# Products on x times its weight beside a norm, and gate weights spread through the merge: one change to a two-block transformer kernel

## The reference

```python
gates = jax.nn.sigmoid(gl + b_merge[l]).reshape(Bn, L, N_BRANCH, D_MODEL)
merged = (gates[:, :, 0] * (y_fox @ w_proj_fox[l])
          + gates[:, :, 1] * (y_s5 @ w_proj_s5[l])
          + gates[:, :, 2] * (y_mem @ w_proj_mem[l]))
x = x + merged @ w_out[l]
...
return rms_norm(x, g_final)          # y = x * rsqrt(mean(x*x) + eps) * g
```

```python
ada = c_act @ w_ada[l] + b_ada[l]
sh1, sc1, gt1, sh2, sc2, gt2 = [a[:, None, :] for a in jnp.split(ada, 6, axis=-1)]
h = rms(x, g_mix[l]) * (1.0 + sc1) + sh1
parts = jnp.split(h @ w_in[l], IN_SPLITS, axis=-1)
...                                   # attention A and B on the parts: y_a, y_b
gate_a = jax.nn.sigmoid(parts[3 + 3 * N_B])
gate_b = jax.nn.sigmoid(parts[4 + 3 * N_B])
x = x + gt1 * ((gate_a * y_a + gate_b * y_b) @ w_out[l])
h2 = rms(x, g_mlp[l]) * (1.0 + sc2) + sh2
x = x + gt2 * (jnp.square(jax.nn.relu(h2 @ w_ff1[l])) @ w_ff2[l])
```

## Time and profile before

| what | value |
|---|---|
| median of three runs | 2289.02 us (2288.14 to 2290.26) |
| profiled execution, its own time | 2291.23 us |
| its span (first to last instruction) | 2289.4 us |
| mean granted TensorE clock | 0.992 |
| instructions | 31094 |
| PE busy | 2249.8 us (98%) |
| POOL busy | 1691.9 us (74%) |
| DVE busy | 1259.3 us (55%) |
| ACT busy | 632.8 us (28%) |

### The profile page before, as it was taken

One profiled execution on the slowest core, in us unless ns is written; L12 is line 12 of the kernel. 1 busy time (PEld: TensorE's weight loads), 2 busy tenths in 40 slices (PEclk: granted clock), 3 DMA queues, 4 the chain that ended last, 5 costly groups with the idle time before them and its releaser, 6 DMA issues.

```text
span 2289.4 us, 31094 instructions
## 1 busy us (share of the span) xinstructions
PE 2249.8 (98%) x11693; PEld 1828.1 (80%) x11693; DVE 1259.3 (55%) x1798; ACT 632.8 (28%) x1286; POOL 1691.9 (74%) x2678
## 2 busy tenths in 40 slices
PE   8999999999999999999999999999999999999999
PEld 6888677788887888777778888878877777888887
DVE  7986345554446665544867576457554456723221
ACT  3233344332224111543223233111144421300000
POOL 7998170867888798344889887889853387899884
PEclk9999999999999899999999999999999999999999
DMA  7456741334455332111545555533321132433221
GB/s 204 129 137 153 268 151 35 116 101 159 159 186 186 111 111 94 50 36 39 164 131 189 174 191 177 184 107 97 100 79 33 29 124 92 154 107 107 92 92 56
DMA packets 268656, 280.87 MB, mean 123 GB/s; under 512 B 29964, under 2 KB 240592, under 8 KB 268508
## 3 DMA queue, kind: packets, MB, share of 16 engines
q1 hardware_dynamic: 249756, 245.86, 34.8%
q10 hardware_dynamic: 18752, 33.03, 4.3%
HBM read 257.87 MB, written 17.85 MB: 120 GB/s over the span
## 4 chain that ended last, share of the span: by engine, by line
PE 85%; POOL 6%; DVE 4%; issue 2%; ACT 2%; DMA 1%; SPq 0%; ACTq 0%; DVEq 0%; POOLq 0%
PE ps L496 46%; PE ps L674 14%; PE ps L2527 4%; PE ps L2528 4%; PE ps L2529 4%; POOL ring_low L272 4%; POOL ring_high L268 3%; PE ps L982 2%; PE ps L1025 2%; PE ps L1001 2%; PE ps L1175 1%; PE ps L1182 1%; PE ps L1158 1%; PE ps L2637 1%; DVE ada_acc L408 1%
## 5 line engine op out<-in xcount | busy, mean ns | idle before, releaser
L272 POOL TENSOR_TENSOR ring_low<-ring,ring_high 128x256 fp32r<-128x256 f32 x1309 | 1039.0, 824 | 28.4
L268 POOL TENSOR_SCALAR ring_high<-ring 128x256 fp32r<-128x256 f32 x1309 | 609.1, 491 | 478.3 <-PE ps L674 170.8
L496 PE MATMUL ps<-hT_high,ring_high 128*128 128x512 f32 x704 | 278.0, 395 | 1.4 <-DVE hT_low L860 1.4
L496 PE MATMUL ps<-hT_low,ring_high 128*128 128x512 f32 x704 | 274.9, 390 | 0.0
L496 PE MATMUL ps<-hT_high,ring_low 128*128 128x512 f32 x704 | 274.0, 389 | 0.0
L674 PE MATMUL ps<-hT_high,ring_high 128*128 128x512 f32 x568 | 234.5, 413 | 3.2 <-POOL ring_low L272 1.4
L674 PE MATMUL ps<-hT_high,ring_low 128*128 128x512 f32 x568 | 225.3, 397 | 0.0
L674 PE MATMUL ps<-hT_low,ring_high 128*128 128x512 f32 x568 | 225.1, 396 | 0.0
L408 DVE TENSOR_REDUCE ada_acc<-ring 128x256 f32<-128x2048 f32 x48 | 188.8, 3933 | 54.8 <-ACT ring L395 54.7
L496 PE MATMUL ps<-hidden_high,ring_high 128*128 128x512 f32 x512 | 201.0, 393 | 0.0
L496 PE MATMUL ps<-hidden_low,ring_high 128*128 128x512 f32 x512 | 199.6, 390 | 0.0
(11 more groups left out here) (401 smaller groups left out, 4030.5 us busy)
## 6 DMA issues: line engine op xcount, KB each, us to landing
ring<-in_w_in_dram SPq DMA_DIRECT2D x75, 1024.0 KB, 5.3
ring<-in_w_ff_dram SPq DMA_DIRECT2D x64, 1024.0 KB, 5.4
ring<-in_w_ada_dram SPq DMA_DIRECT2D x48, 1024.0 KB, 5.4
ring<-in_w_out_dram SPq DMA_DIRECT2D x12, 1024.0 KB, 5.8
scratch_x<-xT ACTq DMA_DIRECT2D x3, 2048.0 KB, 8.2
ring<-in_w_mem_kv_dram SPq DMA_DIRECT2D x4, 1024.0 KB, 5.4
ring<-in_w_branch_a_dram SPq DMA_DIRECT2D x16, 256.0 KB, 4.0
xT<-scratch_x ACTq DMA_DIRECT2D x2, 2048.0 KB, 9.7
```

The costliest lines, as they stand in the source:

```text
L268: ins = nc.gpsimd.tensor_scalar(x(hi), x(raw), 1.0, 1.0, ALU.mult, ALU.mult)
L272: ins = nc.gpsimd.tensor_tensor(x(lo), x(raw), x(hi).bitcast(F32), ALU.subtract)
L496: return nc.tensor.matmul(out[0:rows, bank, cols[0]:cols[1]], lhsT, rhs, start=start, stop=stop)
```

## The change

In the stage ahead of each norm, ACT and DVE also write x times its weight (its gain), without the root, as high and low parts into `hT` (class `Unnormed`). `norm_stage` lets PE multiply the first tile of the stage behind the norm by these; at the double norm it is two tiles. Beside each block's products stand two small products of the same weights with the shift's high and low part, in two columns (`shift_of`). Turn and spread are put between the blocks. When DVE has made the normed blocks, it scales the finished tiles by the spread root; the shift's sum is added as a bias by ACT's tanh or relu. The dummy products go, and the sums are turned in one bank with fewer matmuls.

The first tiles are those of gate slab `m{l}0ga`, which moves ahead of the qkv slabs, and at the MLP norms the first of ff. In layer 1 the second gate tile runs beside the first group of qkv. So the stream has 14 tiles for 16, and the paces are lower: attention A is fed 8 matmuls a step for 9, attention B 10 for 14.

Ada slabs move: the merge gets five more (iterations 3, 5, 7, 9 and 11, between gate and branch slab, keyed to the gate slab's first half) and `ada_lag` 2; out of the first block keeps two of four, out of layer 0 none of three. In out, the sums of squares are added ahead of a tile, not behind it. Mix doesn't wait for the whole stream at its entry, only ahead of its fourth tile. At the MLP norm the normed blocks pass through two PSUM banks instead of SBUF.

The core of the diff:

```diff
@@ -348,27 +348,31 @@
     for mp in range(4):
         for b, (pw, rows) in enumerate((("w_proj_fox", 768), ("w_proj_s5", 768), ("w_proj_mem", 512))):
             add(f"merge{mp}{b}g", w, dm, O_GL + D * b, D, part=mp)
+            one = (len(K.slabs) - 1, 1)
+            if 3 * mp + b in (3, 5, 7, 9, 11):
+                ada(0, 0)
             add(f"merge{mp}{b}p", T[pw][0], (0, rows), 0, D, part=mp)
-            one, other = (len(K.slabs) - 2, 1), (len(K.slabs) - 1, 0)
...
             ada(0)
     for i in range(4):
         add("out", T["w_out"][0], dm, 0, D, part=i)
-        ada(0)
+        if i < 2:
+            ada(0)
...
+        add(f"m{l}0ga", w2, dm, 3072, D, part=0)
...
-            add(f"m{l}{mp}ga", w2, dm, 3072, D, part=mp)
+            if mp:
+                add(f"m{l}{mp}ga", w2, dm, 3072, D, part=mp)
...
         for i in range(4):
             add(f"out{l}", T["w_out_2"][l], dm, 0, D, part=i)
-            if l == 0 and i < 3:
-                ada(0)
...
+    v, hi = K.nc.vector, K.shift_two[:, :, 0]
+    K.link(e, "dve_step", v.tensor_copy(hi, shift))
+    K.link(e, "dve_step", v.tensor_tensor(K.shift_two[:, :, 1], shift, hi.bitcast(F32), ALU.subtract))
+
...
+class Unnormed:
...
+    def round_up(self, e, k):
+        K = self.K
+        K.nc.scalar.activation(K.hT[0][:, k, :], self.src[:, k, :], ACT.Copy, scale=self.gain[:, k:k + 1]
+                               ).then_inc(self.high.sem, 1)
+    def low_part(self, e, k):
+        K = self.K
+        e.wait_ge(self.high.sem, self.base + k + 1)
+        K.nc.vector.scalar_tensor_tensor(K.hT[1][:, k, :], self.src[:, k, :], self.gain[:, k:k + 1],
+                                         K.hT[0][:, k, :].bitcast(F32), ALU.mult, ALU.subtract).then_inc(self.low.sem, 1)
...
+            def products_of(k):
+                pe.wait_ge(unnormed.low.sem, unnormed.base + k + 1)
+                for n, t in enumerate(tiles):
+                    if k == 0:
+                        K.weight_here(pe, t[0][5])
+                    for x in range(3 * k, 3 * k + 3):
+                        _, rows, cols, lhsT, rhs, _, start, stop = t[x]
+                        ins = nc.tensor.matmul(ps[0:rows, tile_banks[n], cols[0]:cols[1]], lhsT, rhs, start=start, stop=stop)
+                ins.then_inc(used.sem, 1)
+            def shift_of(n, k):
+                for x in (3 * k, 3 * k + 2):
+                    ins = nc.tensor.matmul(ps[:, shift_bank, 2 * n:2 * n + 2], tiles[n][x][3], K.shift_two[:, k, :],
+                                           start=x == 0, stop=x == 3 * KD - 1)
+                if (n, k) == (len(tiles) - 1, KD - 1):
+                    ins.then_inc(made.sem, len(tiles))
+            def turn(bank, parts):
+                for t in range(TT):
+                    for n, x in enumerate(parts):
+                        ins = nc.tensor.matmul(ps[:, bank, t:t + 1], x[:, t * P:(t + 1) * P], K.ones[:, 0:1],
+                                               start=n == 0, stop=n == len(parts) - 1)
+                ins.then_inc(turned.sem, 1)
...
+            pe.wait_ge(taken.sem, taken.total - 2)
+            for k in range(KD):
+                products_of(k)
+                if twice is not None:
+                    squared, summed = twice[0]
+                    for h in (2 * k, 2 * k + 1):
+                        shift_of(h // KD, h % KD)
+                    if k == 1:
+                        pe.wait_ge(taken.sem, taken.total)
+                        pe.wait_ge(summed.sem, summed.total)
+                        pe.wait_ge(squared.sem, squared.total - 1)
+                        turn(turn_bank, (sums, last))
+                    if k == 3:
+                        pe.wait_ge(inverted.sem, i0 + 1)
+                        spread_root(root_bank, 4)
+                    if k == 4:
+                        pe.wait_ge(squared.sem, squared.total)
+                        turn(other_bank, (twice[3], twice[4]))
+                    if k == 6:
+                        pe.wait_ge(inverted.sem, i0 + 2)
+                        spread_root(other_bank, 1)
+                else:
+                    shift_of(0, k)
+                    if k == 2:
+                        pe.wait_ge(taken.sem, taken.total)
+                        turn(turn_bank, (sums, last))
+                    if k == 4:
+                        pe.wait_ge(inverted.sem, i0 + 1)
+                        spread_root(root_bank, 4)
...
+                pe.wait_ge(copied.sem, c0 + 1)
...
             low_part(KD - 1)
+            K.link(e, "dve_step", v.tensor_copy(rstd[:, :], ps[:, root_bank, :]))
+            e.wait_ge(made.sem, made0 + len(tiles))
+            for n in range(len(tiles)):
+                K.link(e, "dve_step", v.tensor_reduce(K.shift_of[:, n:n + 1], ps[:, shift_bank, 2 * n:2 * n + 2], AX_X, ALU.add))
+                take(e, n, ps[:, tile_banks[n], :], rstd[:, :])
...
     tiles_stage(K, merge_tiles(K, branches, 4, names), 2, act=act, dve=dve, tensor_entry={}, entry_at=(2, tensor_entry),
-                waits=waits)
+                waits=waits, ada_lag=2)
...
+    unnormed = Unnormed(K, xq, K.gains[:, 3, :])
+    def first_gains(e, n):
+        if n == 0:
+            mix_gains(K, e, 0)
...
+        if n >= 1:
+            unnormed.low_part(e, n - 1)
...
+                if g == 1:
+                    pe.wait_ge(*gates_scaled)
...
                             pe.wait_ge(arriving[0].sem, arriving[1] + k + 1)
+                        if g == 0 and beside is not None and k < KD // 2:
+                            if k == 0:
+                                K.weight_here(pe, beside[0][0][5])
+                            for j in (2 * k, 2 * k + 1):
+                                pe.wait_ge(arriving[0].sem, arriving[1] + j + 1)
+                                for _, _, _, lhsT, rhs, _, start, stop in beside[0][3 * j:3 * j + 3]:
+                                    ins = nc.tensor.matmul(K.ps[:, beside[1], :], lhsT, rhs, start=start, stop=stop)
+                            if k == KD // 2 - 1:
+                                ins.then_inc(beside[2], 1)
...
+    for n in range(2):
+        K.weight_used((gate_slab, n), gates_made.sem, gates_made.total + n + 1)
+    def scale_gates(e, n, ps, rstd):
+        v.tensor_tensor(scaled_gates[n][:, :], ps, rstd, ALU.mult)
+        v.tensor_scalar(K.half_shift[:, n:n + 1], K.shift_of[:, n:n + 1], 0.5, None, ALU.mult).then_inc(gates_scaled.sem, 1)
...
     if l == 0:
-        xq, squared, sums, last = K.outer
-        arriving = norm_stage(K, xq, gains[:, 3, :], K.hT, ada[:, 0:8], sums[1], last[1],
-                              (squared, K.g_final, K.xT, sums[0], last[0]), banks=(2, 3, None))
+        places = ((1, 2), 4, 0, 3, 5, None)
+        xq, unnormed, squared, sums, last = K.outer
+        arriving = norm_stage(K, xq, gains[:, 3, :], K.hT, ada[:, 0:8], sums[1], last[1], unnormed, first_gates, places,
+                              gates_made, scale_gates, (squared, K.g_final, K.xT, sums[0], last[0]))
     else:
...
-            tiles += column_tiles(K, K.first[f"m{l}{mp}g{b}"], 2, KD, K.hT)
-
...
+            if mp or b == "b":
+                tiles += column_tiles(K, K.first[f"m{l}{mp}g{b}"], 2, KD, K.hT)
+    stream = Stream(K, tiles, [(6, 5, 7)[(n + 1) % 3] if n < 9 else 6 + n % 2 for n in range(14)],
+                    lambda e, n, ps: nc.scalar.activation(gates[n + 2], ps, ACT.Tanh, scale=0.5))
...
+    def turn_gates(e):
+        e.wait_ge(gates_scaled.sem, gates_scaled.total)
+        for n in range(2):
+            shift = {"bias": K.half_shift[:, n:n + 1]} if n < ahead else {}
+            nc.scalar.activation(gates[n], scaled_gates[n][:, :], ACT.Tanh, scale=0.5, **shift).then_inc(gates_turned.sem, 1)
...
     attention_stage(K, steps, [probs[:, k] for k in range(4)], [turned[:, k] for k in range(2)], gate_slab, stream,
-                    [72 + 9 * i for i in range(18)] + [240, 252])
+                    [72] + [85 + 8 * i for i in range(17)] + [220, 226])
...
     wide_attention_stage(K, steps, [probs[:, k] for k in range(3)], [t[:, :, :] for t in turned], stream,
-                         [(252, 252, 274)] + [(278 + 14 * i, 284 + 14 * i, 288 + 14 * i) for i in range(7)] + [(376, 382, 384)])
+                         [(226, 226, 246)] + [(249 + 10 * i, 254 + 10 * i, 256 + 10 * i + 8 * (i == 6)) for i in range(7)] + [(328, 334, 336)])
...
-    tiles_stage(K, tiles, 2, dve=mix_dve, also=mix_high, waits={(0, 0): (al.sem, al0 + 4), (0, 12): (yl.sem, yl0 + 2)})
+    tiles_stage(K, tiles, 2, dve=mix_dve, also=mix_high, tensor_entry={x: y for x, y in before.items() if x != "stream"},
+                entry_at=(3, {"stream": before["stream"]}), waits={(0, 0): (al.sem, al0 + 4), (0, 12): (yl.sem, yl0 + 2)})
...
     def mlp_gain(e, n):
-        if n == KD - 1:
...
+        else:
+            unnormed.low_part(e, n - 1)
...
+    def out_high(e, n):
+        if n < KD - 1:
+            e.wait_ge(added.sem, added0 + n + 1)
```

(32 more changed lines are left out.)

180 lines of the change are left out of this document (95 added, 85 removed).

## The result

The changed kernel takes 2296.68 us (median of 20 executions, 2291.04 to 2300.80) against 2289.69 for the kernel before (2286.22 to 2292.38): a ratio of 1.0028, 95% interval 1.0021 to 1.0035, so slower by some 6.5. The forecast was 2286 with a range from 2271 to 2296, so the median lies 0.7 above the range, and the time moved the other way. The changed kernel's profiled execution took 2291.04, the least of the twenty, with a span of 2289.3, hardly other than before (2289.4). I therefore took two more profiles of the same kernel; the third execution (2295.22) is nearest to the median, and the text reads both.

The account below looks back on a forecast made before the run. PE, busy for 98% of the span, was taken as the bound, with gaps at the norms. Gains of 21.3 against 18.5 for moved ada slabs gave -2.8 on 2291.23, taken over to the median 2289.02: 2286 us, range 2271 to 2296.

Parts of the forecast that it names:

- MLP norm, layer 1: Layer 1's MLP norm: the same gain as in layer 0, with its half-clock gap, -4.0 us.
- the price of the moved ada slabs: Merge and out: regular ada slabs wait in the three-slot ring for POOL's gate split; 18.5 us lost, between 8 and 24.
- The falls of the clock: Lower clock after long waits: 2.8 us at merge iteration 5; the second out sum's 5.2 also included a fall.
- The upper bound of 24: Upper end of the forecast loss from the moved ada slabs in merge and out, taken as 18.5 us.
- The double norm: Between out and qkv: gate, shift, turn and spread products fill PE's gap; new stretch 19.8 us, gain 8.6.
- Layer 1's norm: Norm of layer 1's mix: gap of 6.66 becomes 9.9 us, second gate tile beside qkv; net +0.2.
- Layer 0's MLP norm: Tile 0 done in the gap, normed blocks some 1.9 later, tile 2 ends at 21.05 for 24.95: -3.9 us.
- Layer 0's out: Loses its three ada slabs, with a POOL wait of 2.2 and three sums at 0.25: -2.9 us.
- Attention and the entry of mix: Thinner filler costed at nothing in A, B's last step -0.6 us; mix no longer waits for the last gate, -1.5.
- (B): Merge has more slack, landing or split some 3 us sooner: loss 8 for 18.5, 2275 to 2276 us; chance 0.24.
- (C): POOL becomes the bound at the norms, slowed by DVE's low-part passes: 9 us in all, 2295; chance 0.16.
- (D): Attention loses its cover with fewer filler products a step: some 3 us a layer, 2292; chance 0.10.

Follow-up runs that it names:

- the dummy products: The changed kernel with dummy products of 256 columns (4, 7, 4 and 8) ahead of the merge's four long waits for ada sums: 2296.24 us.
- the order of the slabs: The changed kernel with the five extra ada slabs issued ahead of their gate slab, not behind it: 2289.86 us, ratio to before 0.9998.
- the kernel with the ada slabs nearly where they were: Changed kernel, two extra ada slabs in merge (iterations 5, 11, ahead of gate slab), three in layer 0's out, its MLP norm as before: 2285.26 us, ratio 0.9976.

## Why the prediction failed, step by step

The prediction's terms and what they measured, as differences of the table above (first profile, third):

| term | predicted | first | third |
|---|---|---|---|
| merge and out | +18.5 | +23.4 | +25.4 |
| double norm, layer 0's attention and entry of mix | -9.65 | -11.1 | -9.3 |
| out, layer 0 | -2.9 | -3.2 | -3.25 |
| MLP norm, layer 0 | -3.9 | -3.1 | -1.7 |
| norm, attention, entry of mix, layer 1 | -0.85 | -1.3 | -1.2 |
| MLP norm, layer 1 | -4.0 | -4.3 | -4.4 |
| sum | -2.8 | +0.3 | +5.7 |

**The step that failed is the price of the moved ada slabs:** 18.5 in the sum, 23.4 and 25.4 measured. Its mechanism was right, chain and place: iteration 5 was put at a wait of 4.6 and waited 4.3 to 4.6 in three profiles. But iterations 3 and 9 waited 2.7 to 2.8 and 2.5 to 2.6 for 1.3 and 1.4, iteration 11 kept 4.7 to 5.6 *and* a wait of 2.27 at the start of out, where I had set the one off against the other, and the second sum of out waited 2.4 to 2.7. That is 4.7 of waits short in the first profile, of a miss of 4.9. The falls of the clock I added on top, 2.8 twice; for the one in the merge the dummy products show that this was the wrong kind of term: taking the falls away there gave nothing back. I priced wait by wait, each from its own starting tile; the dummy products and the order of the slabs speak for a ring, in which a late slab makes the next one late. The upper bound of 24 was closer than the value taken.

**The double norm** came out as worked out in the first profile: 20.18 where 19.8 stood, of which 0.99 is a wait for POOL and the rest PE's own work:

```profile
765.30 0.39 PE L827 MATMUL ps<-hT_high,ring_low 128*128 128x512 f32 x1
766.68 0.50 PE L827 MATMUL ps<-hT_high,ring_high 128*128 128x512 f32 x1 [0.99 <-POOL ring_low L272]
...
767.25 0.39 PE L827 MATMUL ps<-hT_high,ring_low 128*128 128x512 f32 x1
767.48 0.16 PE L833 MATMUL ps<-shift_two,ring_high 128*128 128x2 f32 x1
...
767.84 0.48 PE L827 MATMUL ps<-hT_high,ring_high 128*128 128x512 f32 x1
```

Four shift products and the start of the next block's product take 0.36 + 0.09, so 0.11 each, at the 0.12 that was taken from the nearest row. The Trainium skill, "TensorE: Matmul & The Clock Gate", section "Wait — 56ns, not 53.3ns?", has a floor of about 25 ns for small matmuls; the rows are over four times that. What I left out: in two of three profiles the clock falls in the middle of this stretch, and of layer 0's MLP norm, and they are 1.4 to 1.9 longer each. Layer 1's norm was put at 9.9 at clock 1; up to the first product of the tile beside qkv it is 11.1 to 11.4 in the three profiles, with a fall in each, and 9.6 in the kernel with the ada slabs nearly where they were, where the clock stays at 1.00.

**Layer 0's MLP norm** began as forecast: PE takes up tiles 1 and 2 at 9.6 after out and the normed blocks come without the delays of before. By the end of tile 2 the first profile had gained 24.95 - 20.7 = 4.2; 1.1 of it went later in ff, 0.85 in a wait for POOL at the first product of ff's ninth tile (0.61 and 0.73 in the other two profiles), which the kernel before doesn't have:

```profile
1215.46 0.47 PE L500 MATMUL ps<-hT_high,ring_high 128*128 128x512 f32 x1 [0.85 <-POOL ring_low L272]
```

The other two profiles lost 1.4 more with the fall.

**Layer 0's out** agrees within 0.4. **Attention and the entry of mix** gain 2.8 and 3.0 a layer, beyond the 10.88 of the two gate tiles that left, where 1.05 stood: the waits on B's probabilities, 1.5 a layer, were put at 0.3, and "PE waits nowhere in A" was misread, for each layer's A had a wait of 0.6. That the table's row for layer 1 agrees within 0.5 is luck: its norm with qkv loses 1.7 for 0.2, by the fall, and attention makes up for it.

**From one execution to the median.** I took the difference in the profiled execution over whole. The first profile after would have given 2289.5 in that way (2289.69 - 0.19); the median is 7 above. The changed kernel's executions spread over 10 us, those of before over 6: in three profiles, new waits of varying length and a fall of the clock in some of the new norms account for most of the differences. The range should have had a term for that on the upper side alone.

**The rivals.** (B), smaller waits, is refuted by three profiles. (C), POOL as the bound at the norms, gave the right sign for a wrong reason: PE waits 1.0 to 1.25 at the first gate products in the three profiles, not 3 to 4 with a fall. But the margin is small. In the profiles of two kernels with the same double norm, the one with the sums three tiles later and the one with two extra slabs in iterations 2 and 8, the wait is 2.6 and 2.5, the clock stands at its lower level for 14 and 10 us behind it, and the double norm takes 28.2 and 28.1 for 20.2:

```profile
772.23 0.80 PE L827 MATMUL ps<-hT_high,ring_high 128*128 128x512 f32 x1 [2.63 <-POOL ring_low L272]
```

```profile
750.85 0.50 PE L986 MATMUL ps<-hT_high,ring_high 128*128 128x512 f32 x1 [2.53 <-POOL ring_low L272]
```

Both are the slowest executions of their kernels (2302.94 and 2290.91), so this wait may also stand behind the slow end of the changed kernel's executions; no profile of it shows that. The Trainium skill, "SBUF — State Buffer", section "SBUF: two separate sides", whose lock would have brought it about, agrees in a smaller place: the MLP norms' low parts, which now read PSUM for one operand, take 0.74 to 0.75 each where up to 1.15 was seen before. (D) didn't come.

**Open:** why iteration 5's slab lands at 6.6 to 7.1 in the kernel with dummies and at 5.2 to 5.5 without, while iteration 11's does so at 7.0 in the kernel without shift products, which has no dummies; and whether the small products or the turn of the sums let the clock fall in the norms. For the turn speaks that in all profiles of the kernels with the new norms each fall in a norm (23 in eleven profiles), but for those at a wait of 2.5 or more, begins 0.2 to 1.5 after a turn has ended, in the kernel without shift products too; but many turns have no fall behind them, and no run leaves a turn out.

## What to carry to other kernels

Work that an edit moves to make room, here five slabs of another job, is part of the edit and has to be priced as a loop: find the slot that each transfer waits for and follow it through two rounds, since a wait filled or a clock kept in a loop that the arrivals pace gives nothing back. When the new form needs its factor early, ask which of its places can have it for nothing; here three of four norms could, and keeping the old form in the fourth, so that three of the five slabs could stay out of the merge, made a loss of 6 into a gain of 5. And a sum against one profiled execution says nothing of the spread: a change that adds waits or stretches of tiny products adds to the median what it adds in only some executions.

## What was not expected of the hardware

The granted clock falls while PE never stands idle: 0.83 over 780 to 790 with PE busy for 10.00 of it, in the second profile of the changed kernel, where PE goes from shift products and sums (one and two columns each) to full products. In the timeline the full product's duration goes from 0.40 to 0.63 with no idle time before it:

```profile
783.48 0.36 PE L841 MATMUL ps<-const,square 128*128 128x1 f32 x2
...
784.25 0.40 PE L827 MATMUL ps<-hT_high,ring_low 128*128 128x512 f32 x1
...
784.72 0.54 PE L827 MATMUL ps<-hT_low,ring_high 128*128 128x512 f32 x1
785.05 0.63 PE L827 MATMUL ps<-hT_high,ring_low 128*128 128x512 f32 x1
```

Behind a true wait of 4.5 it falls as well. With dummy products of 256 columns ahead of the wait, 2.9 to 3.4 of which are left, it stays at 1.00 through the whole merge in one profile; in the other it falls once there, behind such a wait of 2.9 (0.99 over the merge).
